# Expert outputs summed in four PSUM banks over all experts, and tokens gathered by fp32 products from a permuted copy of h

## The reference, cut to what matters

```
h = h + mixed @ w_out
xt = rms_norm(h, ln2_w)
top_val, top_idx = top_k(xt @ w_router + b_router, 4)      # of 32 experts
gate = softmax(top_val)
for each expert e, for the tokens sent to it:
    hu = xt[tokens] @ w_up[e] + b_up[e]                    # 1024 -> 2048
    x_glu = min(hu[:, :1024], 7); x_lin = clip(hu[:, 1024:], -7, 7)
    y = (x_glu * sigmoid(1.702 * x_glu) * (x_lin + 1)) @ w_down[e] + b_down[e]
    h[tokens] += gate * y
output = rms_norm(h)
```

## Time and profile before

| | |
|---|---|
| median of three runs | 1251.53 us |
| span of the profiled execution | 1248.5 us |
| PE busy | 1169.1 us (94%) |
| DVE, ACT busy | 445.6 us (36%), 250.3 us (20%) |
| HBM read | 455.35 MB |

### The profile page before, as it was taken

How to read it: one execution, slowest core, us unless ns; L and a number is a source line. 1 busy time by engine, 2 the same in 40 slices (tenths; PEclk the granted TensorE clock), 3 DMA queues, 4 the chain that set the end, 5 groups by cost and what they waited for, 6 DMA issues and landing times.

```text
span 1248.5 us, 17019 instructions
## 1 busy us (share of the span) xinstructions
PE 1169.1 (94%) x7215; PEld 604.2 (48%) x7216; DVE 445.6 (36%) x766; ACT 250.3 (20%) x353; POOL 15.9 (1%) x30
## 2 busy tenths in 40 slices
PE   9999999999999999899899989898989989899997
PEld 9998988888633343333333333333333333333332
DVE  5754546666532233222222222222322222222232
ACT  4544445544401010001000000000000001000012
POOL 2200000000000000000000000000000000000000
PEclk9999999999999999999999999999999999999999
DMA  9645333377999999999999999999999999999996
GB/s 296 219 169 186 135 135 135 135 277 282 371 417 425 431 431 427 430 430 429 431 433 427 431 430 429 430 430 434 433 428 431 433 427 431 435 427 432 421 428 278
DMA packets 50031, 456.98 MB, mean 366 GB/s; under 512 B 5988, under 2 KB 6136, under 8 KB 31400
## 3 DMA queue, kind: packets, MB, share of 16 engines
q1 hardware_dynamic: 49544, 455.09, 87.7%
q10 hardware_dynamic: 448, 1.32, 0.3%
HBM read 455.35 MB, written 1.05 MB: 366 GB/s over the span
## 4 chain that ended last, share of the span: by engine, by line
PE 59%; DMA 35%; DVE 2%; SPq 2%; ACT 1%; issue 1%; DVEq 0%
PE ps L1384 57%; DMA ring<-in_w_up_dram 22%; DMA arena<-in_w_up_dram 12%; PE ps L1891 1%; DMA ring<-in_w_in_dram 1%; ACT w_split L588 0%; SPq L397 0%; DVE w_split L892 0%; SPq L399 0%; PE ps L1777 0%; PE ps L1573 0%; SPq L414 0%; DVE arena L1062 0%; SPq L391 0%; PE ps L1680 0%
## 5 line engine op out<-in xcount | busy, mean ns | idle before, releaser
L1384 PE MATMUL ps<-ring,arena 128*64 128x512 f32 x2304 | 523.2, 608 | 50.9 <-DMA ring<-in_w_up_dram 50.9
L1384 PEld LDWEIGHTS ps<-ring,arena 128*64 128x64 f32 x2304 | 163.9, 140 | 378.8 <-issue 300.3
L1384 PE MATMUL ps<-arena 128*64 128x512 f32 (+3 forms) x920 | 202.7, 563 | 17.0 <-DMA arena<-in_w_up_dram 16.1
L1296 DVE TENSOR_SCALAR arena<-ps 128x512 f32<-128x512 f32 x32 | 22.1, 692 | 487.3 <-PE ps L1384 487.3
L892 DVE TENSOR_TENSOR w_split<-ring,w_split 128x2048 fp32r<-128x2048 f32 x48 | 109.8, 2291 | 108.4 <-ACT w_split L588 108.1
L1384 PEld LDWEIGHTS ps<-arena 128*64 128x64 f32 (+1 forms) x920 | 78.2, 149 | 128.4 <-issue 100.2
L796 ACT ACTIVATE arena<-arena 128x512 f32<-128x512 f32 x32 | 20.2, 631 | 552.6 <-DVE arena L1296 552.6
L1384 PE MATMUL ps<-w_split,x_split 128*128 128x512 f32 x528 | 123.5, 392 | 0.7 <-ACT arena L624 0.5
L1384 PEld LDWEIGHTS ps<-w_split,x_split 128*128 128x128 f32 x528 | 98.4, 188 | 21.8 <-issue 1.2
L588 ACT ACTIVATE w_split<-ring 128x2048 fp32r<-128x2048 f32 x47 | 89.6, 1911 | 70.7 <-PE ps L1384 62.5
L1384 PE MATMUL ps<-x_split,w_split 128*128 128x256 f32 x768 | 94.7, 284 | 0.1
(11 more groups left out here) (251 smaller groups left out, 624.8 us busy)
## 6 DMA issues: line engine op xcount, KB each, us to landing
ring<-in_w_up_dram SPq DMA_DIRECT2D x40, 4096.0 KB, 31.1
ring<-in_w_down_dram SPq DMA_DIRECT2D x46, 2048.0 KB, 30.2
arena<-in_w_up_dram SPq DMA_DIRECT2D x14, 4096.0 KB, 31.1
ring<-in_w_in_dram SPq DMA_DIRECT2D x17, 2048.0 KB, 7.8
arena<-in_w_down_dram SPq DMA_DIRECT2D x14, 2048.0 KB, 30.0
ring<-in_w_up_dram SPq DMA_DIRECT2D x12, 2048.0 KB, 23.1
arena<-in_w_up_dram SPq DMA_DIRECT2D x4, 2048.0 KB, 23.5
ring<-in_w_up_dram SPq DMA_DIRECT2D x8, 1024.0 KB, 8.7
```

The costliest lines, as they stand in the source:

```text
L1296: dve.tensor_scalar(glu_c, ps[bank][:, :], LIMIT, None, ALU.min).then_inc(glu_ok, 1)
L1384: return pe.matmul(dst, lhsT, rhs, start=start, stop=stop, skip_group_check=True)
```

## The change

- `h_rows`, a permuted fp32 copy of h that isn't scaled, takes the place of `xs2` and `xs2p`; two ACT copies make it, and the splits are gone. `sel` becomes fp32 and carries the reciprocal root. `gather` is 8 x 2 fp32 products, into bank 2 (shared with `act_transposed`).
- `scatter` writes for both token tiles into the four banks of `SUM_BANK`, which accumulate from step 1 of the first turn to the end. The adds on DVE, `scat_ps` and `scat_ok` are gone. All eight products come ahead of the gather; the first step has none.
- `one_hot_transposed` uses bank 0 in place of 5.
- At the end, h itself is brought into the four banks by one fp32 product each with `ident`; `h_high`, `h_low`, `ident_r` are gone.
- New or moved waits on PE: `xin_ok` ahead of the hidden transposes, `selT_out` ahead of the up bias, `actT_ok` ahead of the gather, `glu_ok` ahead of `one_hot_transposed`.

```diff
-                act.wait_ge(h2_rstd, t + 1)
-                act.activation(xs2[:, t, :].rearrange("q (c s p) -> q c s p", c=2, s=4),
-                               h_sb[:, t, :].rearrange("q (c p s) -> q c s p", c=2, s=4), ACT.Copy,
-                               scale=rstd[:, t:t + 1]).then_inc(xs2_ok, 1)
-                act.wait_ge(xs2_ok, t + 1)
-                act.activation(xs2p[:, 0, t, :], xs2[:, t, :], ACT.Copy).then_inc(hi_ok, 1)
+                act.activation(h_rows[:, t, :].rearrange("q (c s p) -> q c s p", c=2, s=4),
+                               h_sb[:, t, :].rearrange("q (c p s) -> q c s p", c=2, s=4), ACT.Copy).then_inc(h_rows_ok, 1)
...
-            for t in range(TT):
-                act.wait_ge(res_ok[t], 1)
-                act.activation(xs2p[:, 1, t, :], xres[t], ACT.Copy).then_inc(mid_ok, 1)
-            for t in range(TT):
-                act.wait_ge(low_ok[t], 1)
...
-                    dve.tensor_scalar(sel[:, t, :], slot_no[:, 0:CAP], slots[:, t, bass.ds(n, 1)], None,
-                                      ALU.is_equal).then_inc(sel_ok, 1)
+                    dve.tensor_scalar(sel[:, t, :], slot_no[:, 0:CAP], slots[:, t, bass.ds(n, 1)], rstd[:, t:t + 1],
+                                      ALU.is_equal, ALU.mult).then_inc(sel_ok, 1)
...
                 glu_half()
-                add_last_share(i, u, (0, 1))
                 hidden(at_n(2), i * (PER_DVE * UNROLL) + PER_DVE * (u + 2))
                 dve.wait_ge(xin_ps, at_n(3))
                 gathered(u % 2)
-                add_last_share(i, u, (2, 3))
...
                 for k in range(KT):
-                    for n in range(PIECES * TT):
-                        ins = mm(ps[4][:, k * CAP:k * CAP + CAP], xs2p[:, n // TT, n % TT, k * P:k * P + P],
-                                 sel[:, n % TT, :], n == 0, n == PIECES * TT - 1)
+                    for t in range(TT):
+                        ins = mm(ps[2][:, k * CAP:k * CAP + CAP], h_rows[:, t, k * P:k * P + P], sel[:, t, :],
+                                 t == 0, t == TT - 1)
...
-            def scatter(n4, par, t):
-
-                if t:
-                    pe.wait_ge(scat_ok, n4 + 2)
-                for piece in range(2):
-                    for half in range(2):
-                        rows = slice(half * CAP, half * CAP + CAP)
-                        ins = mm(ps[6 + half][:, :], selT[rows, par, t * P:t * P + P], y_split[rows, piece, :],
-                                 piece == 0, piece == 1)
+            def scatter(par, t, piece, first=False):
+
+                for half in range(2):
+                    rows = slice(half * CAP, half * CAP + CAP)
+                    mm(ps[SUM_BANK[2 * t + half]][:, :], selT[rows, par, t * P:t * P + P], y_split[rows, piece, :],
+                       first and piece == 0, False)
...
-                pe.wait_ge(h_low_ok, q + 1)
                 t, cols = q // 2, slice((q % 2) * 512, (q % 2) * 512 + 512)
-                mm(ps[SUM_BANK[q]][:, :], ident_r[:, :], h_high[:, t, cols], True, False)
-                mm(ps[SUM_BANK[q]][:, :], ident_r[:, :], h_low[:, t, cols], False, False)
+                mm(ps[SUM_BANK[q]][:, :], ident[:, :], h_sb[:, t, cols], False, False)
...
+                pe.wait_ge(xin_ok, at_n(2))
                 if not first:
                     act_transposed(at_n(1))
-                pe.wait_ge(xin_ok, at_n(2))
+                    pe.wait_ge(selT_out, at_n(0))
                 pe.wait_ge(pick_ok, at_n(3))
...
-                pe.wait_ge(y_ok, at_n(1))
-                pe.wait_ge(selT_ok, at_n(1))
-                scatter(i * (4 * UNROLL) + 4 * u, (u + 1) % 2, 0)
+                if not first:
+                    pe.wait_ge(y_ok, at_n(0))
+                    pe.wait_ge(selT_ok, at_n(1))
+                    for t in range(TT):
+                        for piece in range(2):
+                            scatter((u + 1) % 2, t, piece, starts)
                 pe.wait_ge(sel_ok, i * (TT * UNROLL) + TT * (u + 2))
+                pe.wait_ge(actT_ok, at_n(1))
                 gather()
+                pe.wait_ge(glu_ok, at_n(2))
                 one_hot_transposed(i * (TT * UNROLL) + TT * (u + 1))
-                scatter(i * (4 * UNROLL) + 4 * u, (u + 1) % 2, 1)
```

More of the change, by code:

```diff
@@ L140, in layer @@
         gk2_sb = arena[0:RANK, T0 + 3328:T0 + 3328 + 512]
-        xs2p = at(0, 3072).bitcast(BF16).rearrange("p (n t c) -> p n t c", n=PIECES, t=TT)
-        xs2 = at(TMP0, 2048).rearrange("p (t c) -> p t c", t=TT)
-        xres = [at(TMP0 + 2048, D), at(M0, D)]
+        h_rows = at(0, 2048).rearrange("p (t c) -> p t c", t=TT)
         place = [3072]
@@ L218, in layer @@
         turns_i = sb("turns_i", [1, 2], I32)
-        sel = sb("sel", [P, TT, CAP], BF16)
+        sel = moe(TT * CAP).rearrange("p (t s) -> p t s", t=TT)
         g_slot = sb("g_slot", [P, 2])
@@ L257, in layer @@
             sem(n) for n in ("sig_ok", "o_ssq", "o_root", "o_norm", "obT_ps", "obT_ok"))
-        h2_ok, h2_ssq, h2_root, h2_rstd, xs2_ok, x2T_ps, x2T_ok = (
-            sem(n) for n in ("h2_ok", "h2_ssq", "h2_root", "h2_rstd", "xs2_ok",
+        h2_ok, h2_ssq, h2_root, h2_rstd, h_rows_ok, x2T_ps, x2T_ok = (
+            sem(n) for n in ("h2_ok", "h2_ssq", "h2_root", "h2_rstd", "h_rows_ok",
                              "x2T_ps", "x2T_ok"))
-        hi_ok, mid_ok = sem("hi_ok"), sem("mid_ok")
-        low_ok = [sem(f"low_ok{t}") for t in range(TT)]
-        res_ok = [sem(f"res_ok{t}") for t in range(TT)]
         wo_half, part_ok, sel0_ok, xin_half_ps, xin_half_ok, warmed = (
@@ L274, in layer @@
             sem(n) for n in ("glu_ok", "sig_done", "act_ok", "actT_ps", "actT_ok"))
-        y_out, y_ok, scat_ps, scat_ok = (sem(n) for n in ("y_out", "y_ok", "scat_ps", "scat_ok"))
+        y_out, y_ok = sem("y_out"), sem("y_ok")
         last_root, stored = sem("last_root"), sem("stored")
@@ L278, in layer @@
         last_rstd, out_ok = sem("last_rstd"), sem("out_ok")
-        ident_r_ok, h_high_ok, h_low_ok, sum_ps, last_sq, scaled_ok, normed_ok = (
-            sem(n) for n in ("ident_r_ok", "h_high_ok", "h_low_ok", "sum_ps", "last_sq", "scaled_ok", "normed_ok"))
+        sum_ps, last_sq, scaled_ok, normed_ok = (
+            sem(n) for n in ("sum_ps", "last_sq", "scaled_ok", "normed_ok"))
         SUM_BANK = (6, 7, 4, 5)
@@ L562, in _ @@
             pool.memset(selT[:, 1, :].bitcast(F32), 0.0).then_inc(selT_ok, 1)
-            pool.memset(y_split[:, :, :].bitcast(F32), 0.0).then_inc(y_ok, 1)
         @block.scalar
@@ L783, in _, with one_hot_out @@
             last_turn = act.value_load(turns_i[0:1, 0:1], min_val=TURNS - 1, max_val=TURNS * MAX_ROUNDS - 1)
-            def one_hot_out(n1, par, bank=5):
+            def one_hot_out(n1, par, bank=0):
                 act.wait_ge(selT_ps, n1)
@@ L822, in _ @@
             act.activation(actT, ps[2][:, :], ACT.Copy).then_inc(actT_ok, 1)
[L823 to L828, removed]
             sigmoid(n_last(4))
@@ L1253, in _ @@
                    .then_inc((xin_half_ok, xin_ok)[half], 1)
[L1254 to L1259, removed]
             dve.wait_ge(lg_exp, 1)
@@ L1282, in _ @@
             last_turn = dve.value_load(turns_i[0:1, 0:1], min_val=TURNS - 1, max_val=TURNS * MAX_ROUNDS - 1)
[L1284 to L1292, removed]
             def glu_half(bank=0):
@@ L1344, in _ @@
             choose_gated(n_last(2))
[L1345 to L1349, removed]
             dve.wait_ge(chunk_used, last_turn * TURN_CHUNKS + up_end(UNROLL - 2))
@@ L1821, in first_up @@
                         pe.wait_ge(sel_ok, TT)
-                        for t in range(TT):
-                            pe.wait_ge(low_ok[t], 1)
+                        pe.wait_ge(h_rows_ok, TT)
                         gather()
@@ L1895, in h_kept @@
             def h_kept(q):
-                pe.wait_ge(h_low_ok, q + 1)
                 t, cols = q // 2, slice((q % 2) * 512, (q % 2) * 512 + 512)
-                mm(ps[SUM_BANK[q]][:, :], ident_r[:, :], h_high[:, t, cols], True, False)
-                mm(ps[SUM_BANK[q]][:, :], ident_r[:, :], h_low[:, t, cols], False, False)
-            def share_kept(par, piece, t):
-                for half in range(2):
-                    rows = slice(half * CAP, half * CAP + CAP)
-                    mm(ps[SUM_BANK[2 * t + half]][:, :], selT[rows, par, t * P:t * P + P], y_split[rows, piece, :],
-                       False, False)
+                mm(ps[SUM_BANK[q]][:, :], ident[:, :], h_sb[:, t, cols], False, False)
             def last_share(piece, t):
@@ L1916, in last_share, with expert_pe @@
                         ins.then_inc(sum_ps, 1)
-            def expert_pe(i, u, first=False, halves_landed=False, late=None):
+            def expert_pe(i, u, first=False, halves_landed=False, late=None, starts=False):
                 def at_n(k):
@@ L1950, in _ @@
             for u in range(UNROLL):
-                expert_pe(0, u, first=u == 0, halves_landed=u == 1)
```

(17 more changed lines are left out.)

11 lines of the change are left out of this document (2 added, 9 removed).

## The result

The changed kernel takes 1257.63 us (median of 6 runs), the kernel before 1251.89 us (6 runs). The ratio is 1.0053, with a 95% interval of 1.0038 to 1.0069: slower by 0.5%. The profiled execution spans 1255.5 us against 1248.5, 7.0 us more; the medians differ by 5.7 us, since the kernel before was profiled in an execution that was shorter than its median.

A forecast was written before the change was run, and what follows sets the result against it. The DMA stream of weights was taken to bound the loop. Start 3.7 plus tail 5.0 gave 8.7 us on a span of 1248.5, 1257.2 us; with 3.03 us from span to median, 1260.2 us, range 1255 to 1264.

The forecast's parts named there:

- The bound: In the loop, the DMA stream of weights bounds: period 29.2 us, PE waiting about 1.2 us per expert after the change.
- The gather: On PE, each expert's gather: 32 fp32 records take 4.0 us instead of 1.41, +2.6 us, covered in the loop.
- nearer the 64-column row: In the gather's estimate: 4.0 us chosen from 3.8 to 4.1, nearer the first gather's 0.128 us per record.
- The rival by columns: In the gather: fp32 products cost only their streaming, 1.8 us a gather, total 1252.7 us; chance 0.07.
- The adds and splits at 0, the moved waits at 0: Dropped DVE adds, dropped splits of h on ACT and DVE, and moved waits on PE: each changes the time by 0.
- The rival of a DMA that gains from the adds that go: In the loop's stream: without the adds' SBUF traffic DMA runs faster, 1.4% giving about 1248 us; chance 0.05.
- The start of the stream: At SP's first pair issue, 3.9 us later at 378.5: the DMA queue runs dry, +3.7 us (2.8 to 4.5).
- The step that counted a reserve of 1.1 us and a restart of 1.7 us: At the stream's start: 0.5 MB queued bridges 1.1 us of the delay; issuing into an empty queue loses 1.7 us.
- the start is absorbed: At the stream's start: the queue bridges the later issue and only the tail remains, 1256.5 us; chance 0.12.
- The tail: After PE's last wait: 1.6 us late at the last chunk, one gather +2.6, `h_kept` +0.8; together +5.0 us (4.4 to 5.4).
- the step that took four paired records of 128x64 as the price of one full-width product: In the tail's `h_kept`: one fp32 product of 512 columns priced at 0.87 us from four up-product records.
- PE as the bound in the loop: In the loop: half-clock gathers make PE's period 32.0 us, 27 experts paying 2.7 each, about 1330 us; chance 0.03.

The follow-up runs named there:

- banks_only: The changed kernel with the old bf16 gather put back, its other parts kept: 1251.98 us, ratio 1.0004 to the kernel before.
- gather_only: The kernel before with only the gather changed to fp32 products: 1256.67 us, ratio 1.0041 to the kernel before.
- gather_behind_down: The changed kernel with the gather of step 0 moved behind the first down products: 1259.95 us, ratio 1.0072 to the kernel before.
- h_turn0: The changed kernel with h brought into the four banks in step 3 of the first turn, not in the tail: 1254.27 us, ratio 1.0029.
- delay3: The kernel before with 3.0 us of idle products (14) behind the gather of first_up: 1253.77 us, ratio 1.0024 to the kernel before.
- h_turn0_bf16: The changed kernel with h brought in during step 3 of the first turn and the bf16 gather put back: 1249.68 us, ratio 0.9997.

## Why the prediction was right, and where its sizes were off

**The bound** held: period 29.22 us, one wait per expert once PE has caught up, 431 GB/s. The waits were 1.8 us where 1.2 were forecast, since the gather is shorter and the scatter in one row saves 0.2 us. The half-clock stretches of the loop went with the longer waits, as forecast (granted clock 1.00 for 0.97).

**The gather**: 4.0 us forecast, 3.62 measured. The step took 0.128 us a record, "nearer the 64-column row"; the in-loop record takes 0.113, below even the router's 0.118, so between 32 and 64 columns their number plays no part, which leaves the load of the weights as the price (at 512 columns it is otherwise: 0.53 us a record in `h_kept`). The rival by columns (1.8 us) falls. The Trainium skill, "TensorE: Matmul & The Clock Gate", section "Weight-path perf modes — Fast Weight Load (FWL) and DoubleRow", says that fast weight load is off for fp32. The gathers agree: 0.029 us a record in bf16, 0.113 in fp32.

**The adds and splits at 0, the moved waits at 0**: right, by banks_only. Only `y_split`'s 0.99 us is left among PE's waits for another engine behind 343 us, as before. The rival of a DMA that gains from the adds that go falls: 431 GB/s for 430, and the same period.

**The start of the stream**: +3.7 forecast, +1.5 at the last landing, less than the term's own lower end of 2.8. The mechanism was right, three of its sizes were not. The issue came at 377.58, not 378.5 (the shorter gather). The step that counted a reserve of 1.1 us and a restart of 1.7 us makes a delay cost 0.6 us more than its length; the bytes lag 0.2 to 0.5 us less than it, and the queue ran thin at 350 us too. How large each of the two is was not measured, only that they nearly cancel. The window of the earlier trace rows, from which the restart was priced, opens at 325.00 us, half a us ahead of the issue at 325.48, and so counts the draining queue too. And of the 2.7 us by which the changed kernel's bytes are late, about 1.2 don't reach the landing, as the surplus behind it is 0.92 MB instead of 1.4 to 1.5 (0.5 MB at 430 GB/s). The prediction had no such term. What sets the surplus early, between 500 and 575 us, stays open. The runs show that a longer program raises it, and that it is lower with the fp32 gather (0.9 to 1.1 MB at the last landing in the changed kernel, gather_only, gather_behind_down and h_turn0) than with the bf16 gather (1.3 to 1.7 in the kernel before, banks_only, delay3 and h_turn0_bf16). The rival "the start is absorbed" is refuted by delay3.

**The tail**: +5.0 forecast, +4.5 measured. 1.05 and 2.0 for the gathers (1.6 and 2.6 forecast), 1.4 for `h_kept` (0.8 forecast). There the step that took four paired records of 128x64 as the price of one full-width product was low: 1.05 us instead of 0.87.

**The stores**: nothing forecast, +1.0 measured. The prediction had no term behind the last products.

**The sum**: 8.7 us forecast on the span, 7.0 measured. The offset from span to median was 2.1 us for 3.0, which brings the median to 1257.6 instead of 1260.2, within the range. The 3.0 us weren't a constant: where a run's time stands beside its own span, it is 1.7 to 2.6 us longer, and the rest came from the short execution in which the kernel before was profiled. Luck is in this total: the start was overrated by 2.2 us, while 1.0 us in the stores was not foreseen. And 1257.63 lies nearer to the rival with the absorbed start (1256.5) than to the forecast; only delay3 and the count of bytes tell that the start was not absorbed. PE as the bound in the loop never came near: full clock, 1.8 us of wait.

## What to carry to other kernels

Where a stream of weights at full share sets the pace, ask of an edit only what it does ahead of the stream's first issues and behind the last wait: 2.2 us more in each gather cost nothing in some 27 experts, but 1.5 us at the start and 3 us in the tail. Count matmul records by what limits them, here the load of 128x128 fp32 weights at 0.11 us against 0.03 in bf16, not by their number alone. And test a queue's reserve by putting a plain delay into the old kernel before trusting a byte count: here delays of 3 and 6 us cost 2.7 and 5.6 us of stream.

## What was not expected of the hardware

A turn of the loop written out, with no other work, cost 2.8 us of span: 8 instruction packets from 680 to 900 us, landings 3.1 us later by the end (1163.79 for 1160.71), the bytes moved only some 0.5 us further behind. Two kernels whose bytes lag equally (2.7 us) can thus wait for the same chunk at times 1.7 us apart (1160.71 in the changed kernel, 1162.37 in delay3). And the half clock behind a wait isn't decided by the wait alone: behind 2.63 to 2.65 us a pair took 7.09 us in one expert of the kernel before and 8.78 in another, with a granted clock of 1.00 from 574.67 to 577 us and of 0.57 from 603.93 to 606.

```profile
574.67 7.09 PE L1384 MATMUL ps<-ring,arena 128*64 128x512 f32 x32 [2.63 <-DMA ring<-in_w_up_dram]
...
603.93 8.78 PE L1384 MATMUL ps<-ring,arena 128*64 128x512 f32 x32 [2.65 <-DMA ring<-in_w_up_dram]
```
